# Second attention's scores and values and the pooling's grouped projection as three passes of split operands

## The chip, the cores and the metric

The kernel runs on one core of a Trainium2 chip. The metric is the time on the device of one execution, in microseconds: 1687.03 as the median of three runs (1686.83 to 1687.77). Lower is better.

## The reference, cut to what matters

Two transformer layers follow each other over 256 tokens of width 2048, all in f32. The change touches two parts of the second layer: the windowed attention's two products, and the linear map of the pooling branch.

```python
def windowed_gqa(q, k, v, rel_table, sink):      # 8 query heads, 2 key heads, width 128
    ...
    logits = jnp.einsum('bnqkgd,bntkd->bnkgqt', qb, kw).astype(jnp.float32) * (HEAD_DIM_2 ** -0.5)
    ...
    probs = jax.nn.softmax(jnp.concatenate([logits, sink_l], axis=-1), axis=-1)[..., :-1]
    out = jnp.einsum('bnkgqt,bntkd->bnqkgd', probs.astype(vw.dtype), vw)

def multiscale_pool(u, w_grp, scale):            # 4 groups of 256 channels, windows 2, 4, 8, 16
    ...
    pooled = jnp.stack(outs, axis=2).astype(u.dtype)
    mixed = jnp.einsum('bsgc,gcd->bsgd', pooled, w_grp).reshape(B, S, POOL_WIDTH)
    return mixed * scale

def hybrid_layer(...):
    proj = h @ w_in
    q, k, v, gate_a, u, gate_p = jnp.split(proj, SPLIT_POINTS, axis=-1)
    y_a = windowed_gqa(q, k, v, rel_table, sink) * jax.nn.silu(gate_a)
    y_p = multiscale_pool(u, w_pool_grp, pool_scale) * jax.nn.silu(gate_p)
    ...
```

## The kernel before, in words

All large products read f32 weights from HBM. A "sub" is a piece of 256 rows by 512 columns of one weight matrix. SyncE loads it (tile `raw`, 8 buffers); ScalarE copies it into the reduced format f32r (`w_hi`, 4 buffers, L1158); VectorE subtracts that copy from it (`w_lo`, L1442); and TensorE multiplies in three passes, high by high, high by low and low by high (L726 and its neighbours). The activations have been split in the same way (`X_pair`, `Y_pair`).

Five phases follow each other: P1 (first layer's mixing), P2 (its MLP), P3 (second layer's input projection, 72 subs in nine blocks of eight), P4 (merge) and P5 (output). In P3 each sub is 24 passes of 256 columns into the PSUM tile `G`, whose two halves take the blocks in turn. Between the subs stand small "stages" that use the other PSUM tile, `S`. The list `STAGES` gives each a slot (after which sub it comes) and the number of steps that each engine has in it. Each engine walks the same list by itself: at slot s, ScalarE and VectorE first convert sub s + 3 (`AHEAD` = 3) and then do their part of the stages of slot s, strictly in order; TensorE multiplies sub s and then does its part. A w_hi can be written when TensorE is done with the sub four before it. `enter` makes an engine wait until all other engines have finished all steps of the stages that stand before this one in the list.

The stages that matter here, by slot:

- `inb0` (7), `inb1` (15), then `inb2`, `inb3` with the second and third score stage (24, 31), `inb4` (40): ScalarE copies a finished block out of `G`: keys and values, queries (two blocks), pooling inputs `u` (two blocks). `inb5` (47) is a Silu of the attention's gate.
- `gate_sum` (8): small matmuls of the gate vector.
- Four rounds (half of the tokens by four heads each): `win_L` (17, 24, 31, 38), the scores, L1104, then scaling, bias and maximum on VectorE; `win_E` the exponentials on ScalarE; `win_M` the sum on VectorE; `win_S` (five slots after win_L), eight transposes of the probabilities into two banks of `S` (L707), one bank copied out by ScalarE (L1382) and one by VectorE (L1793) side by side; `win_V` (one slot later), the values, L1117, copied to `ya` (L1804).
- `pool_0` to `pool_3` (45, 46, 47, 49): window sums on VectorE (L1816 to L1825). GpSimd loads the group weights `w_grp` (1 MB) when it enters pool_0.
- `pool_W` (53): the grouped projection, sixteen f32 matmuls of 256 columns, L1124; it waits for `w_grp`.

A plain f32 matmul is one instruction in the program:

```python
ins = nc.tensor.matmul(S[:, k // 2, TOK * (k % 2):TOK * (k % 2 + 1)],
                       q2_T[:, h0 + k, P * tt:P * (tt + 1)], k2_T[:, (h0 + k) // 4, :], start=True, stop=True)
```

The profile leaves out buffer numbers in names: q2_T is q_T there, v2 is v, probs2_T is probs_T.

Of the kernel before, what the change touches and what calls it, by code (L numbers as in the profile page):

```python
# [27 lines left out]
P = 128  # L28
# [240 lines left out]
stage("P3", 0, "h2_scale", D=4)  # L269
for _k in range(4):  # L270
    stage("P3", 2 + _k, f"h2_T{_k + 1}", P=1, A=1, D=2)
stage("P3", 7, "inb0", A=1)
stage("P3", 8, "gate_sum", P=1, D=1)
stage("P3", 9, "gate_row", P=1, D=1)
stage("P3", 10, "x_fin0", D=1)
stage("P3", 12, "x_fin1", D=1)
stage("P3", 15, "inb1", A=1)
stage("P3", 16, "u_pads", G=1)
for _g, _s in enumerate((17, 24, 31, 38)):
    stage("P3", _s, f"win_L{_g}", P=1, D=4)  # L280
    if _g in (1, 2):
        stage("P3", _s, f"inb{_g + 1}", A=1)
    stage("P3", _s + 2, f"win_E{_g}", A=2)
    if _g == 3:
        stage("P3", 40, "inb4", A=1)
    stage("P3", _s + 3, f"win_M{_g}", D=3)
    stage("P3", _s + 5, f"win_S{_g}", P=1, A=1, D=1)
    stage("P3", _s + 6, f"win_V{_g}", P=1, D=1)
stage("P3", 45, "pool_0", D=3)
stage("P3", 46, "pool_1", D=4)  # L290
stage("P3", 47, "pool_2", D=5)
stage("P3", 47, "inb5", A=1)
stage("P3", 49, "pool_3", D=6)
stage("P3", 53, "pool_W", P=1, A=1, D=1)
stage("P3", 55, "inb6", A=1)
stage("P3", 56, "ya0", A=1, D=2)
stage("P3", 57, "ya1", A=1, D=2)
# [51 lines left out]
def program(nc, t, out):  # L349
# [4 lines left out]
    with ctx:  # L354
# [89 lines left out]
        y_n, _ = put("y_n", X_AT, [P, NT, D_MODEL])  # L444
        tmp_T, _ = put("tmp_T", X_AT + 16 * KB, [P, 4, NW])
        bias2, at2 = put("bias2", X_AT, [P, NT, Q_HEADS2, TOK])
        q2_T, at2 = put("q2_T", at2, [P, Q_HEADS2, TOK])
        k2_T, at2 = put("k2_T", at2, [P, KV_HEADS2, TOK])
        probs2, at2 = put("probs2", at2, [P, 4, TOK])
        w_grp, _ = put("w_grp", X_AT + 16 * KB, [P, 4, 2, PGW])  # L450
        assert at2 <= X_AT + 32 * KB
        ya, at = put("ya", AR, [P, Q_HEADS2, TOK])
        v2, at = put("v2", at, [P, NT, KV_HEADS2 * P])
        probs2_T, at = put("probs2_T", AR + 12 * KB, [P, 4, 2, P])
        ga, at = put("ga", at, [P, 8, TOK])
        yp, _ = put("yp", at, [P, 8, TOK])
        u, at = put("u", at, [P, 8, PAD + TOK + PAD])
        gp, at = put("gp", at, [P, 8, TOK])
        sums, at = put("window_sums", at, [P, 2, 2, PAD + TOK + PAD])
        assert at <= AR + 48 * KB  # L460
        pool_edge, _ = put("pool_edge", AR + 10 * KB, [P, 4, 2, PAD])

        sig, at = put("sig", AR, [P, 2, 4, TOK])
# [241 lines left out]
        def _(pe):  # L705
# [90 lines left out]
                need("P1", OUT_AT + 10 + k, "D", step("D", "mix_T2", k + 1))  # L796
            need("P1", OUT_AT + 16, "D", done("D", "out0"))
            need("P1", OUT_AT + 24, "D", done("D", "out1"))
            for b in range(9):
                if b >= 2:  # L800
                    need("P3", 8 * b, "A", done("A", f"inb{b - 2}"))
            for k in range(8):
                need("P3", k, "D", halves_made(2 * k) if k < 4 else done("D", f"h2_T{k - 3}"))
            need("P5", 0, "G", done("G", "br_p", QUARTERS - 2))
# [102 lines left out]
            def stages(name, i):  # L907
# [158 lines left out]
                elif name == "gla_F":  # L1066
                    for tt in range(NT):
                        for h in range(GLA_HEADS):
                            ins = nc.tensor.matmul(S[:, tt, P * h:P * (h + 1)], ki_T[:, tt, h, :], qd_T[:, tt, h, :],
                                                   start=True, stop=True)  # L1070
                    ins.then_inc(pe_side, 1)
                elif name[:5] == "gla_G":
                    for h in range(GLA_HEADS):
                        v = 2 * GW + GLA_DV * h
                        for n in ((0, 1) if name == "gla_G01" else (2,)):
                            tt, r = n // 2, slice(GLA_CHUNK * (n % 2), GLA_CHUNK * (n % 2 + 1))
                            b0 = 2 * ((n + 1) % 2)
                            ins = nc.tensor.matmul(S[0:GLA_DK, b0 + h // 2, GLA_DV * (h % 2):GLA_DV * (h % 2 + 1)],
                                                   gla[r, tt, GW + GLA_DK * h:GW + GLA_DK * (h + 1)],
                                                   gla[r, tt, v:v + GLA_DV], start=True, stop=True)  # L1080
                    ins.then_inc(pe_side, 1)
                elif name == "gla_O":
                    for tt in range(NT):
                        for h in range(GLA_HEADS):
                            v = 2 * GW + GLA_DV * h
                            c_ = slice(GLA_DV * (h % 2), GLA_DV * (h % 2 + 1))
                            b_ = 2 * tt + h // 2
                            nc.tensor.matmul(S[:, b_, c_], sc_T[:, tt, h, :], gla[:, tt, v:v + GLA_DV],
                                             start=h % 2 == 0, stop=False, skip_group_check=True)
                    for n, h in [(n, h) for h in range(GLA_HEADS) for n in (1, 2)] + [(3, h) for h in range(GLA_HEADS)]:  # L1090
                        tt, r = n // 2, slice(GLA_CHUNK * (n % 2), GLA_CHUNK * (n % 2 + 1))
                        c_ = slice(GLA_DV * (h % 2), GLA_DV * (h % 2 + 1))
                        ins = nc.tensor.matmul(S[r, 2 * tt + h // 2, c_], qd_T[:, tt, h, r], state[:, n - 1, h, :],
                                               start=False, stop=True, skip_group_check=True)
                    ins.then_inc(pe_side, 1)
                elif name == "gate_sum":
                    fold(S[:, 0, 0:KC], 2 * KC, KC)
                elif name == "gate_row":
                    swap(S[0:KC, 1, 0:P], gate_v[:, :]).then_inc(pe_side, 1)
                elif name[:5] == "win_L":  # L1100
                    g = int(name[-1])
                    tt, h0 = g % 2, 4 * (g // 2)
                    for k in range(4):
                        ins = nc.tensor.matmul(S[:, k // 2, TOK * (k % 2):TOK * (k % 2 + 1)],  # L1104
                                               q2_T[:, h0 + k, P * tt:P * (tt + 1)], k2_T[:, (h0 + k) // 4, :],
                                               start=True, stop=True)
                    ins.then_inc(pe_side, 1)
                elif name[:5] == "win_S":
                    for k in range(4):
                        for kt in range(2):  # L1110
                            ins = swap(S[:, k // 2, TOK * (k % 2) + P * kt:TOK * (k % 2) + P * (kt + 1)],
                                       probs2[:, k, P * kt:P * (kt + 1)])
                    ins.then_inc(pe_side, 1)
                elif name[:5] == "win_V":
                    g = int(name[-1])
                    for kt in range(2):
                        ins = nc.tensor.matmul(S[:, 2, :], v2[:, kt, P * (g // 2):P * (g // 2 + 1)], probs2_T[:, :, kt, :],  # L1117
                                               start=kt == 0, stop=kt == 1)
                    ins.then_inc(pe_side, 1)
                elif name == "pool_W":  # L1120
                    pe.wait_ge(grp_in, 16)
                    for k in range(8):
                        for c in range(2):
                            ins = nc.tensor.matmul(S[:, k // 2, TOK * (k % 2):TOK * (k % 2 + 1)],  # L1124
                                                   w_grp[:, k // 2, c, P * (k % 2):P * (k % 2 + 1)],
                                                   u[:, 2 * (k // 2) + c, PAD:PAD + TOK], start=c == 0, stop=c == 1)
                    ins.then_inc(pe_side, 1)
                else:
                    raise AssertionError(name)
# [13 lines left out]
        def _(act):  # L1143
# [44 lines left out]
            def stages(name, i):  # L1188
# [41 lines left out]
                elif name[:3] == "inb":  # L1230
# [3 lines left out]
                    G1 = G[:, (b + 1) % 2, 1, :].rearrange("p (c q) -> p c q", q=TOK)  # L1234
                    both = G[:, (b + 1) % 2, :, :].rearrange("p a (c q) -> p (a c) q", q=TOK)
                    if b == 0:
                        nc.scalar.activation(k2_T[:, :, :], G0, ACT.Copy)
                        ins = nc.scalar.activation(v2[:, :, :], G1, ACT.Copy)
                    elif b < 3:
                        ins = nc.scalar.activation(q2_T[:, 4 * (b - 1):4 * b, :], both, ACT.Copy)  # L1240
                    elif b < 5:
                        ins = nc.scalar.activation(u[:, 4 * (b - 3):4 * (b - 2), PAD:PAD + TOK], both, ACT.Copy)
                    else:
# [135 lines left out]
                    nc.scalar.activation(small[:, 48:52], small[:, 24:28], ACT.Exp).then_inc(act_side, 1)  # L1379
                elif name[:5] == "win_S":  # L1380
                    act.wait_ge(pe_side, done("P", name))
                    nc.scalar.activation(probs2_T[:, 0:2, :, :], S[:, 0, :].rearrange("p (h k q) -> p h k q", h=2, k=2),  # L1382
                                         ACT.Copy).then_inc(act_side, 1)
                elif name == "pool_W":
                    act.wait_ge(pe_side, done("P", name))
                    nc.scalar.activation(yp[:, 0:4, :], S[:, 0:2, :].rearrange("p a (c q) -> p (a c) q", q=TOK),
# [44 lines left out]
        def _(dve):  # L1431
# [83 lines left out]
            def stages(name, i):  # L1515
# [274 lines left out]
                                        bias2[:, g % 2, h0:h0 + 4, ::-1])], probs2[:, :, :], 4, SWA_HEADS + h0, HD2 ** -0.5)  # L1790
                elif name[:5] == "win_S":
                    dve.wait_ge(pe_side, done("P", name))
                    nc.vector.tensor_copy(probs2_T[:, 2:4, :, :], S[:, 1, :].rearrange("p (h k q) -> p h k q", h=2, k=2)  # L1793
                                          ).then_inc(dve_side, 1)
                elif name[:5] == "win_M":
                    softmax_sum(name, 4)
                    dve.wait_ge(dve_side, step("D", name, 2))
# [215 lines left out]
```

## Time and profile before

| what | value |
|---|---|
| device time, median of 3 runs | 1687.03 us |
| span of the profiled execution | 1685.6 us |
| the profiled execution's own device time | not given apart from its span |
| TensorE busy | 1676.8 us (99%) |
| VectorE busy | 1121.0 us (67%) |
| ScalarE busy | 822.0 us (49%) |
| HBM read over the span | 358.00 MB, 214 GB/s |
| P3, about | 1093 to 1324 us |

The span runs from the first to the last instruction in the trace. Busy times are those of an engine's instructions; TensorE's weight loads (PEld) are counted by themselves and lie beside its matmuls. A matmul's record is longer than its share of the engine, since matmuls are pipelined: the distance from one start to the next tells what it costs. A plain f32 matmul is two records.

### The profile page before, as it was taken

The page shows a single profiled execution, that of the slowest core. Times are in us where ns is not written, and L with a number is a line of the kernel's source. Part 1 is how long each engine was busy: PE and PEld are TensorE (multiplying, and loading weights), DVE is VectorE, ACT ScalarE, POOL GpSimd, SP SyncE. Part 2 cuts the span into 40 slices and gives each one's busy share as a digit, 9 for nine tenths or more (in the row PEclk, how much of TensorE's full clock was granted, in tenths as well). Part 3 has the DMA queues.
Part 4 walks back from the last instruction along what each step waited for, and adds up shares of the span by engine and source line. Part 5 has one row for each costly group of instructions (what it writes and reads, how often), then busy time and mean ns, then how long its engine had stood idle before and what let it go on. Part 6 is the DMA issues. An engine that isn't in the chain of part 4 may idle for free.

```text
span 1685.6 us, 25429 instructions
## 1 busy us (share of the span) xinstructions
PE 1676.8 (99%) x9373; PEld 1453.1 (86%) x9373; DVE 1121.0 (67%) x1143; ACT 822.0 (49%) x1084; POOL 56.3 (3%) x63
## 2 busy tenths in 40 slices
PE   9999999999999999999999999999999999999998
PEld 6888888888888888888888888799999988888886
DVE  5454546557877777777877777775575566757754
ACT  5645754554445444454455445454444454444443
POOL 1000000000000000000000000000000001101100
PEclk9999999999999999999999999999999999999999
DMA  8643545467777788767777777675555655555562
GB/s 299 220 136 116 188 138 173 163 206 267 261 257 262 271 277 278 252 233 277 267 265 258 267 254 259 209 243 159 169 169 176 193 189 191 179 195 173 195 205 88
DMA packets 171643, 361.47 MB, mean 214 GB/s; under 512 B 10971, under 2 KB 17435, under 8 KB 171296
## 3 DMA queue, kind: packets, MB, share of 16 engines
q1 hardware_dynamic: 169376, 352.37, 62.7%
q0 software_dynamic: 2032, 7.56, 1.2%
q8 instruction: 65, 1.06, 0.3%
q10 hardware_dynamic: 144, 0.26, 0.0%
q14 instruction: 26, 0.21, 0.0%
HBM read 358.00 MB, written 2.15 MB: 214 GB/s over the span
## 4 chain that ended last, share of the span: by engine, by line
PE 98%; DVE 1%; issue 1%; ACT 0%; POOLq 0%; POOL 0%; ACTq 0%; DVEq 0%
PE G L745 31%; PE S L745 13%; PE S L759 12%; PE G L759 12%; PE G L726 10%; PE G L762 6%; PE S L762 6%; PE S L707 2%; PE G L732 1%; PE S L1124 0%; PE S L1104 0%; PE S L1117 0%; PE S L778 0%; DVE window_sums L1816 0%; PE S L993 0%
## 5 line engine op out<-in xcount | busy, mean ns | idle before, releaser
L1442 DVE TENSOR_TENSOR w_lo<-raw,w_hi 128x1024 fp32r<-128x1024 f32 (+2 forms) x574 | 704.4, 1245 | 414.9 <-ACT w_hi L1158 414.1
L1158 ACT ACTIVATE w_hi<-raw 128x1024 fp32r<-128x1024 f32 (+2 forms) x575 | 589.5, 1045 | 522.3 <-PE G L745 130.7
L745 PE MATMUL G<-w_hi,X_pair 128*128 128x512 f32 (+2 forms) x1472 | 450.0, 384 | 0.1
L745 PEld LDWEIGHTS G<-w_hi,X_pair 128*128 128x128 f32 x1472 | 272.5, 188 | 56.2 <-issue 3.7
L745 PE MATMUL G<-w_lo,X_pair 128*128 128x512 f32 (+2 forms) x736 | 280.0, 380 | 0.0
L759 PE MATMUL S<-Y_pair,w_hi 128*128 128x512 f32 x768 | 267.0, 390 | 0.0
L759 PE MATMUL G<-Y_pair,w_hi 128*128 128x512 f32 x768 | 266.8, 390 | 0.0
L762 PE MATMUL G<-Y_pair,w_lo 128*128 128x256 f32 x768 | 216.6, 282 | 0.0
L762 PE MATMUL S<-Y_pair,w_lo 128*128 128x256 f32 x768 | 216.6, 282 | 0.0
L726 PE MATMUL G<-Y_pair,w_hi 128*128 128x256 f32 x1088 | 196.2, 283 | 1.1 <-DVE Y_pair L1558 0.9
L759 PEld LDWEIGHTS S<-Y_pair,w_hi 128*128 128x128 f32 x768 | 144.1, 188 | 30.3
L759 PEld LDWEIGHTS G<-Y_pair,w_hi 128*128 128x128 f32 x768 | 144.1, 188 | 30.2
L726 PEld LDWEIGHTS G<-Y_pair,w_hi 128*128 128x128 f32 x1088 | 166.3, 188 | 3.7 <-issue 1.9
L745 PEld LDWEIGHTS G<-w_lo,X_pair 128*128 128x128 f32 x736 | 138.4, 188 | 25.8 <-issue 0.5
L745 PE MATMUL S<-w_hi,X_pair 128*128 128x512 f32 x512 | 158.3, 389 | 0.0
L726 PE MATMUL G<-Y_pair,w_lo 128*128 128x256 f32 x544 | 151.7, 279 | 0.0
L762 PEld LDWEIGHTS S<-Y_pair,w_lo 128*128 128x128 f32 x768 | 145.1, 189 | 0.2
L762 PEld LDWEIGHTS G<-Y_pair,w_lo 128*128 128x128 f32 x768 | 145.2, 189 | 0.0
L1455 DVE SCALAR_TENSOR_TENSOR ada_acc<-ada_w,c_silu,ada_acc 128x768 f32<-128x768 f32 x120 | 121.5, 1012 | 0.0
L745 PEld LDWEIGHTS S<-w_hi,X_pair 128*128 128x128 f32 x512 | 96.1, 188 | 20.0
L726 PEld LDWEIGHTS G<-Y_pair,w_lo 128*128 128x128 f32 x544 | 102.2, 188 | 0.0
L745 PE MATMUL S<-w_lo,X_pair 128*128 128x512 f32 x256 | 99.6, 389 | 0.0
(334 smaller groups left out, 1429.0 us busy)
## 6 DMA issues: line engine op xcount, KB each, us to landing
raw<-in_w_in SPq DMA_DIRECT2D x143, 512.0 KB, 4.4
raw<-in_w_mlp_in SPq DMA_DIRECT2D x128, 512.0 KB, 5.4
raw<-in_w_mlp_out SPq DMA_DIRECT2D x128, 512.0 KB, 6.7
ada_w<-in_w_ada SPq DMA_DIRECT2D x64, 768.0 KB, 4.9
raw<-in_w_out SPq DMA_DIRECT2D x64, 512.0 KB, 4.5
raw<-in_w_merge SPq DMA_DIRECT2D x64, 512.0 KB, 4.2
raw<-in_w_branch_attn SPq DMA_DIRECT2D x16, 512.0 KB, 4.1
raw<-in_w_branch_pool SPq DMA_DIRECT2D x16, 512.0 KB, 6.0
```

What stands on the lines that cost most here:

```text
L707: return nc.tensor.transpose(out_, in_, ident)
L726: ins = nc.tensor.matmul(G[:, bank, j // 2, TOK * (j % 2):TOK * (j % 2 + 1)], w[:, s % SPLIT, c, cut], a[:, c0 + c, :], start=first and c ...
L732: ins = nc.tensor.matmul(G[:, bank, 1, TOK * tt:TOK * (tt + 1)], a[:, c0 + c, P * tt:P * (tt + 1)], w[:, s % SPLIT, c, P * turned:NW], sta ...
L745: ins = nc.tensor.matmul(token_bank(bank, tt)[:, 0:n], a[:, c0 + c, tok], w[:, s % SPLIT, c, 0:n], start=first and c == 0 and k == 0, stop ...
L759: nc.tensor.matmul(bank, w_hi[:, s % SPLIT, c, cut], both[:, c0 + c, :, :].rearrange("p a q -> p (a q)"), start=first and c == 0, stop=Fal ...
L762: ins = nc.tensor.matmul(bank[:, 0:TOK], w_lo[:, s % SPLIT, c, cut], both[:, c0 + c, 0, :], start=False, stop=last and c == SUB - 1, skip_ ...
L1158: nc.scalar.activation(w_hi[:, s % SPLIT, :, 0:n], raw[:, k, :, 0:n], ACT.Copy).then_inc(hi_ready, 1)
L1442: nc.vector.tensor_tensor(w_lo[:, s % SPLIT, :, 0:n], raw[:, k, :, 0:n], w_hi[:, s % SPLIT, :, 0:n], ALU.subtract).then_inc(lo_ready, 1)
L1455: nc.vector.scalar_tensor_tensor(a, w, cs[:, v:v + 1], a, ALU.mult, ALU.add).then_inc(ada_free, 1)
```

## The change

The f32 operands of these products are replaced by pairs of f32r tiles, high and low, and each f32 matmul by three passes. ScalarE's copies out of PSUM now write the high tiles, and VectorE gets a step in `inb0`, `inb1` and `inb2` that subtracts them for the low ones. In `win_S` ScalarE copies both banks, and VectorE then subtracts; before, each copied one. Three stages are new: `pool_w` (48) splits the group weights (2048 elements per partition on each engine), `pool_u0` (51) and `pool_u1` (53) split the pooled inputs. `pool_W` moves from slot 53 to 55, and the wait for the load of `w_grp` from TensorE to ScalarE's pool_w. TensorE's blocks 2, 3 and 4 now wait for VectorE's step of the drain. The new tiles lie on space that is free at that time.

```diff
-stage("P3", 7, "inb0", A=1)
+stage("P3", 7, "inb0", A=1, D=1)
...
-stage("P3", 15, "inb1", A=1)
+stage("P3", 15, "inb1", A=1, D=1)
...
-        stage("P3", _s, f"inb{_g + 1}", A=1)
+        stage("P3", _s, f"inb{_g + 1}", A=1, D=2 - _g)
...
+stage("P3", 48, "pool_w", A=1, D=1)
 stage("P3", 49, "pool_3", D=6)
-stage("P3", 53, "pool_W", P=1, A=1, D=1)
+stage("P3", 51, "pool_u0", A=1, D=1)
+stage("P3", 53, "pool_u1", A=1, D=1)
+stage("P3", 55, "pool_W", P=1, A=1, D=1)
...
-            for b in range(9):
-                if b >= 2:
-                    need("P3", 8 * b, "A", done("A", f"inb{b - 2}"))
+            for b in range(2, 9):
+                need("P3", 8 * b, "D" if b < 5 else "A", done("D" if b < 5 else "A", f"inb{b - 2}"))
...
-                        ins = nc.tensor.matmul(S[:, k // 2, TOK * (k % 2):TOK * (k % 2 + 1)],
-                                               q2_T[:, h0 + k, P * tt:P * (tt + 1)], k2_T[:, (h0 + k) // 4, :],
-                                               start=True, stop=True)
+                        for m, (q, keys) in enumerate(((q2_hi, k2_hi), (q2_hi, k2_lo), (q2_lo, k2_hi))):
+                            ins = nc.tensor.matmul(S[:, k // 2, TOK * (k % 2):TOK * (k % 2 + 1)],
+                                                   q[:, h0 + k, P * tt:P * (tt + 1)], keys[:, (h0 + k) // 4, :],
+                                                   start=k % 2 == 0 and m == 0, stop=m == 2, skip_group_check=True)
...
-                        ins = nc.tensor.matmul(S[:, 2, :], v2[:, kt, P * (g // 2):P * (g // 2 + 1)], probs2_T[:, :, kt, :],
-                                               start=kt == 0, stop=kt == 1)
+                        for m, (v, p) in enumerate(((v2_hi, probs2_hi), (v2_hi, probs2_lo), (v2_lo, probs2_hi))):
+                            ins = nc.tensor.matmul(S[:, 2, :], v[:, kt, P * (g // 2):P * (g // 2 + 1)], p[:, :, kt, :],
+                                                   start=kt == 0 and m == 0, stop=kt == 1 and m == 2)
...
-                    pe.wait_ge(grp_in, 16)
                     for k in range(8):
                         for c in range(2):
+                            for m, (w, a) in enumerate(((w_grp_hi, u_hi), (w_grp_lo, u_hi), (w_grp_hi, u_lo))):
...
-                    nc.scalar.activation(probs2_T[:, 0:2, :, :], S[:, 0, :].rearrange("p (h k q) -> p h k q", h=2, k=2),
+                    nc.scalar.activation(probs2_hi[:, :, :, :].rearrange("p (a h) k q -> p a (h k q)", a=2), S[:, 0:2, :],
...
+                elif name == "pool_w":
+                    act.wait_ge(grp_in, 16)
+                    nc.scalar.activation(w_grp_hi[:, :, :, :], w_grp[:, :, :, :], ACT.Copy).then_inc(act_side, 1)
+                elif name in ("pool_u0", "pool_u1"):
+                    k = 4 * int(name[-1])
+                    nc.scalar.activation(u_hi[:, k:k + 4, :], u[:, k:k + 4, PAD:PAD + TOK], ACT.Copy).then_inc(act_side, 1)
...
-                    nc.vector.tensor_copy(probs2_T[:, 2:4, :, :], S[:, 1, :].rearrange("p (h k q) -> p h k q", h=2, k=2)
-                                          ).then_inc(dve_side, 1)
+                    dve.wait_ge(act_side, done("A", name))
+                    nc.vector.tensor_tensor(probs2_lo[:, :, :, :].rearrange("p (a h) k q -> p a (h k q)", a=2), S[:, 0:2, :],
+                                            probs2_hi[:, :, :, :].rearrange("p (a h) k q -> p a (h k q)", a=2),
+                                            ALU.subtract).then_inc(dve_side, 1)
...
+                elif name == "pool_w":
+                    dve.wait_ge(act_side, done("A", name))
+                    nc.vector.tensor_tensor(w_grp_lo[:, :, :, :], w_grp[:, :, :, :], w_grp_hi[:, :, :, :],
+                                            ALU.subtract).then_inc(dve_side, 1)
...
```

VectorE's steps of `inb0` to `inb2`, `pool_u0` and `pool_u1` have the form of the last one: wait for ScalarE's step, subtract.

## Rows read from the trace of the kernel before

**Rows 1.** The page: busy time by engine; the chain of waits by engine.
```profile
PE 1676.8 (99%) x9373; PEld 1453.1 (86%) x9373; DVE 1121.0 (67%) x1143; ACT 822.0 (49%) x1084; POOL 56.3 (3%) x63
...
PE 98%; DVE 1%; issue 1%; ACT 0%; POOLq 0%; POOL 0%; ACTq 0%; DVEq 0%
```

**Rows 2.** Four stretches: us, busy by engine (instructions), PE clock, DMA share, GB/s.
```profile
1148.00:1172.00 24.00, 24.00 (x191) 22.83 (x190) 13.78 (x20) 11.25 (x18) 0.00 (x0) 1.00 0.56 171
1244.00:1254.00 10.00, 10.00 (x88) 10.00 (x87) 8.67 (x14) 2.56 (x3) 0.05 (x1) 1.00 0.82 262
1679.00:1680.00 1.00, 0.00 (x0) 0.00 (x0) 0.69 (x2) 0.08 (x1) 0.56 (x1) 1.00 0.09 33
1683.00:1684.00 1.00, 0.00 (x0) 0.00 (x0) 0.00 (x0) 0.00 (x0) 0.00 (x0) 0.50 1.06 367
```

**Rows 3.** Chain of waits in order of time: start, us, engine, line, count.
```profile
1043.98 43.52 PE G L745 x192
...
1119.39 2.79 PE G L726 x24
...
1148.43 1.73 PE S L1104 x8
...
1165.03 2.81 PE G L726 x24
1167.84 1.72 PE S L1117 x4
...
1267.31 6.91 PE S L1124 x32
```

**Rows 4.** Timeline of PE: start, us, weight loads (PEld) or matmuls, [idle before].
```profile
1167.56 0.31 PEld L1117 LDWEIGHTS S<-probs_T,v 128*128 128x128 f32 x2
...
1264.24 0.30 PEld L726 LDWEIGHTS G<-Y_pair,w_hi 128*128 128x128 f32 x2 [0.41 <-DVE w_lo L1442]
...
1680.38 1.13 PE L1139 MATMUL S<-o_sb,diag 128*128 128x512 f32 x2 [1.52 <-ACT diag L1410]
```

**Rows 5.** Timeline of ACT, attention and pooling.
```profile
1120.00 0.59 ACT L1238 ACTIVATE v<-G 128x512 f32<-128x512 f32 x1
...
1165.15 0.60 ACT L1382 ACTIVATE probs_T<-S 128x512 f32<-128x512 f32 x1 [2.63 <-PE S L707]
...
1254.86 1.03 ACT L1245 ACTIVATE ga<-G 128x1024 f32<-128x1024 f32 x1
1255.78 3.89 ACT L1158 ACTIVATE w_hi<-raw 128x1024 fp32r<-128x1024 f32 x4
```

**Rows 6.** Timeline of DVE, the same stretch.
```profile
1213.30 0.69 DVE L1793 COPY probs_T<-S 128x512 f32<-128x512 f32 x1 [0.76 <-PE S L707]
...
1256.87 2.36 DVE L1442 TENSOR_TENSOR w_lo<-raw,w_hi 128x1024 fp32r<-128x1024 f32 x2 [3.44 <-ACT w_hi L1158]
1259.15 0.72 DVE L1816 TENSOR_TENSOR window_sums<-u 128x542 f32<-128x542 f32 x1
...
1262.97 4.62 DVE L1442 TENSOR_TENSOR w_lo<-raw,w_hi 128x1024 fp32r<-128x1024 f32 x4
```

**Rows 7.** Groups by shape, ACT and DVE: count | busy us, mean ns | idle before.
```profile
L1158 ACT ACTIVATE w_hi<-raw 128x1024 fp32r<-128x1024 f32 x559 | 579.9, 1056 | 516.7 <-PE S L762 126.3 <-PE G L745 125.1 <-PE G L762 119.1
...
L1158 ACT ACTIVATE w_hi<-raw 128x512 fp32r<-128x512 f32 x8 | 4.7, 640 | 2.5 <-PE G L745 2.5
...
L1442 DVE TENSOR_TENSOR w_lo<-raw,w_hi 128x512 fp32r<-128x512 f32 x8 | 5.3, 688 | 5.5 <-ACT w_hi L1158 5.5
...
L1488 DVE SCALAR_TENSOR_TENSOR probs<-S,bias 128x1024 f32<-128x1024 f32 x4 | 4.9, 1226 | 10.5 <-PE S L1104 10.5
...
L1767 DVE SCALAR_TENSOR_TENSOR x_res<-x_res,stat,norm_f 128x2048 f32<-128x2048 f32 x2 | 4.7, 2344 | 0.0
```

**Rows 8.** The load of w_grp: KB, us to landing; its issue on POOL.
```profile
w_grp<-in_w_pool_group POOLq DMA_DIRECT2D x1, 1024.0 KB, 8.0
...
1243.13 0.92 POOL L1897 DMA_DIRECT2D w_grp<-in_w_pool_group  x1 [98.85 <-DVE ya L1804]
```

More of the change, by code:

```diff
@@ L446, in program @@
         bias2, at2 = put("bias2", X_AT, [P, NT, Q_HEADS2, TOK])
-        q2_T, at2 = put("q2_T", at2, [P, Q_HEADS2, TOK])
-        k2_T, at2 = put("k2_T", at2, [P, KV_HEADS2, TOK])
+        q2_hi, at2 = put("q2_hi", at2, [P, Q_HEADS2, TOK], f32r)
+        k2_hi, at2 = put("k2_hi", at2, [P, KV_HEADS2, TOK], f32r)
+        k2_lo, at2 = put("k2_lo", at2, [P, KV_HEADS2, TOK], f32r)
         probs2, at2 = put("probs2", at2, [P, 4, TOK])
+        w_grp_hi, _ = put("w_grp_hi", X_AT, [P, 4, 2, PGW], f32r)
+        w_grp_lo, _ = put("w_grp_lo", X_AT + 8 * KB, [P, 4, 2, PGW], f32r)
         w_grp, _ = put("w_grp", X_AT + 16 * KB, [P, 4, 2, PGW])
@@ L452, in program @@
         ya, at = put("ya", AR, [P, Q_HEADS2, TOK])
-        v2, at = put("v2", at, [P, NT, KV_HEADS2 * P])
-        probs2_T, at = put("probs2_T", AR + 12 * KB, [P, 4, 2, P])
+        v2_hi, at = put("v2_hi", at, [P, NT, KV_HEADS2 * P], f32r)
+        probs2_hi, at = put("probs2_hi", AR + 12 * KB, [P, 4, 2, P], f32r)
         ga, at = put("ga", at, [P, 8, TOK])
@@ L457, in program @@
         u, at = put("u", at, [P, 8, PAD + TOK + PAD])
+        q2_lo, _ = put("q2_lo", at, [P, Q_HEADS2, TOK], f32r)
+        u_hi, _ = put("u_hi", at, [P, 8, TOK], f32r)
         gp, at = put("gp", at, [P, 8, TOK])
         sums, at = put("window_sums", at, [P, 2, 2, PAD + TOK + PAD])
+        v2_lo, at = put("v2_lo", at, [P, NT, KV_HEADS2 * P], f32r)
         assert at <= AR + 48 * KB
+        probs2_lo, _ = put("probs2_lo", AR + 16 * KB, [P, 4, 2, P], f32r)
+        u_lo, _ = put("u_lo", X_AT + 24 * KB, [P, 8, TOK], f32r)
         pool_edge, _ = put("pool_edge", AR + 10 * KB, [P, 4, 2, PAD])
@@ L1116, in stages @@
                     for kt in range(2):
-                        ins = nc.tensor.matmul(S[:, 2, :], v2[:, kt, P * (g // 2):P * (g // 2 + 1)], probs2_T[:, :, kt, :],
-                                               start=kt == 0, stop=kt == 1)
+                        for m, (v, p) in enumerate(((v2_hi, probs2_hi), (v2_hi, probs2_lo), (v2_lo, probs2_hi))):
+                            ins = nc.tensor.matmul(S[:, 2, :], v[:, kt, P * (g // 2):P * (g // 2 + 1)], p[:, :, kt, :],
+                                                   start=kt == 0 and m == 0, stop=kt == 1 and m == 2)
                     ins.then_inc(pe_side, 1)
                 elif name == "pool_W":
-                    pe.wait_ge(grp_in, 16)
                     for k in range(8):
                         for c in range(2):
-                            ins = nc.tensor.matmul(S[:, k // 2, TOK * (k % 2):TOK * (k % 2 + 1)],
-                                                   w_grp[:, k // 2, c, P * (k % 2):P * (k % 2 + 1)],
-                                                   u[:, 2 * (k // 2) + c, PAD:PAD + TOK], start=c == 0, stop=c == 1)
+                            for m, (w, a) in enumerate(((w_grp_hi, u_hi), (w_grp_lo, u_hi), (w_grp_hi, u_lo))):
+                                ins = nc.tensor.matmul(S[:, k // 2, TOK * (k % 2):TOK * (k % 2 + 1)],
+                                                       w[:, k // 2, c, P * (k % 2):P * (k % 2 + 1)], a[:, 2 * (k // 2) + c, :],
+                                                       start=k % 2 == 0 and c == 0 and m == 0, stop=c == 1 and m == 2,
+                                                       skip_group_check=True)
                     ins.then_inc(pe_side, 1)
@@ L1236, in stages @@
                     if b == 0:
-                        nc.scalar.activation(k2_T[:, :, :], G0, ACT.Copy)
-                        ins = nc.scalar.activation(v2[:, :, :], G1, ACT.Copy)
+                        nc.scalar.activation(k2_hi[:, :, :], G0, ACT.Copy)
+                        ins = nc.scalar.activation(v2_hi[:, :, :], G1, ACT.Copy)
                     elif b < 3:
-                        ins = nc.scalar.activation(q2_T[:, 4 * (b - 1):4 * b, :], both, ACT.Copy)
+                        ins = nc.scalar.activation(q2_hi[:, 4 * (b - 1):4 * b, :], both, ACT.Copy)
                     elif b < 5:
@@ L1792, in stages @@
                     dve.wait_ge(pe_side, done("P", name))
-                    nc.vector.tensor_copy(probs2_T[:, 2:4, :, :], S[:, 1, :].rearrange("p (h k q) -> p h k q", h=2, k=2)
-                                          ).then_inc(dve_side, 1)
+                    dve.wait_ge(act_side, done("A", name))
+                    nc.vector.tensor_tensor(probs2_lo[:, :, :, :].rearrange("p (a h) k q -> p a (h k q)", a=2), S[:, 0:2, :],
+                                            probs2_hi[:, :, :, :].rearrange("p (a h) k q -> p a (h k q)", a=2),
+                                            ALU.subtract).then_inc(dve_side, 1)
+                elif name in ("inb0", "inb1", "inb2"):
+                    b = int(name[3:])
+                    dve.wait_ge(act_side, done("A", name))
+                    both = G[:, (b + 1) % 2, :, :].rearrange("p a (c q) -> p (a c) q", q=TOK)
+                    if b == 0:
+                        nc.vector.tensor_tensor(k2_lo[:, :, :], both[:, 0:2, :], k2_hi[:, :, :], ALU.subtract)
+                        ins = nc.vector.tensor_tensor(v2_lo[:, :, :], both[:, 2:4, :], v2_hi[:, :, :], ALU.subtract)
+                    else:
+                        q = slice(4 * (b - 1), 4 * b)
+                        ins = nc.vector.tensor_tensor(q2_lo[:, q, :], both, q2_hi[:, q, :], ALU.subtract)
+                    ins.then_inc(dve_side, 1)
+                elif name == "pool_w":
+                    dve.wait_ge(act_side, done("A", name))
+                    nc.vector.tensor_tensor(w_grp_lo[:, :, :, :], w_grp[:, :, :, :], w_grp_hi[:, :, :, :],
+                                            ALU.subtract).then_inc(dve_side, 1)
+                elif name in ("pool_u0", "pool_u1"):
+                    dve.wait_ge(act_side, done("A", name))
+                    k = 4 * int(name[-1])
+                    nc.vector.tensor_tensor(u_lo[:, k:k + 4, :], u[:, k:k + 4, PAD:PAD + TOK], u_hi[:, k:k + 4, :],
+                                            ALU.subtract).then_inc(dve_side, 1)
                 elif name[:5] == "win_M":
```

## Prediction

> **What bounds the kernel now.** First the busy shares and the chain of waits: TensorE (PE) is busy 99% of the span and makes up 98% of the chain [rows 1]. So time goes only where PE has less to stream, and comes where PE is made to wait. The change lies in the third phase (P3), whose matmuls are 72 "subs" of 24 passes of 256 columns; ScalarE (ACT) makes each sub's w_hi, VectorE (DVE) its w_lo, three subs ahead. The stretches show how much room the helpers have there: in one attention round DVE works 13.8 of 24 us and ACT 11.3, but in the 10 us in which the pooling sums start DVE works 8.7 of 10 [rows 2]. The third view is the timeline around that place. PE has its one wait for w_lo of this phase at 1263.8: weight loads that follow each other by 0.12 us stop and go on at 1264.24, released by DVE [rows 4]. There PE has no slack: it is sub 53, just before the pooling's projection (pool_W). A microsecond more on DVE or ACT in front of that w_lo is a microsecond of PE. The reader is to see both sides: whatever the change saves on PE is certain, whatever it adds to DVE between 1244 and 1263 is paid.
>
> **What PE saves.** In before a plain f32 matmul appears as two records. Eight records of 256 columns (scores, four matmuls) take 1.73 us, four of 512 columns (values, two matmuls) 1.72, and the 32 of pool_W 6.91 [rows 3]. A split pass of 256 columns costs 2.81/24 = 0.117 us, one of 512 columns 43.52/192 = 0.227 [rows 3]. Three passes instead of one f32 product then are:
> scores, 12 passes: 1.41 us, 0.32 less, four times: 1.29;
> values, 6 passes: 1.36 us, 0.36 less, four times: 1.44;
> pool_W, 48 passes: 5.63 us, 1.28 less.
> Together 4.0 us. The small gain on three passes against two double records comes from the pass itself: half a record is 6.91/64 = 0.108 us, a split pass 0.117. Bounds: if a pass cost only that 0.108, the sum would be 12 × 0.108 = 1.30 per scores round and so on, 5.0 us in all; if the first pass after another kind of work lost another 0.1 us in each of the nine places, 3.1. I take 4.0, since the passes are of the very form that surrounds them.
> The Trainium skill ("FP8 and Floating Point Precision", TensorE Precision Notes) says that true FP32 takes four passes through the array; three for four would save a quarter of 1.73 × 4 + 1.72 × 4 + 6.91 = 20.7 us, 5.2 us. By that rule alone the net below would be 2.3 us faster instead of 1.2; the rows, where a lone pass costs more than a quarter of an f32 product, decide.
>
> **What is added where it is hidden.** (1) Block drains inb0 to inb2: DVE now subtracts behind ACT's copies, two of 512 elements (0.69 us each) and two of 1024 (1.23) [rows 7]. inb0 is the nearest: ACT's copy ends at 1120.59 [rows 5], the two subtractions by 1121.9, and PE's next side stage, gate_sum, which now waits for them too, follows sub 8 at 1122.18 [rows 3]; 0.25 us to spare. inb1 has two subs (5.6 us) before the first scores, for 1.03 + 1.23. inb2 waits behind the softmax maximum as its copy did already. What is queued behind, w_lo for three subs ahead, moves by 0.2 to 0.3. If such a cover is gone, PE waits the difference once. Bounds 0 and 0.3; I take 0. PE's own new waits (blocks 2 to 4 on DVE) come eight subs after the drain: nothing.
> (2) win_S, four times: today ACT and DVE each copy 512 elements of the turned probabilities side by side; now ACT copies 1024 (1.03, as q_T and ga) and DVE subtracts 1024 after it (1.23). From the end of the transposes at 1165.03: ACT starts 1165.15 [rows 5], ends 1166.18, DVE 1166.21 to 1167.43. PE wants the result when the loads of the values begin, 1167.56 [rows 4]. The handoff DVE to PE took 0.05 in the wait above, so 0.08 us is left. DVE is free at that time (0.76 idle before the copy where it was least [rows 6]) and the next w_hi and w_lo behind it have three subs of room. Bounds: 0, and 4 × 0.2 = 0.8 us lost if each handoff is 0.1 to 0.3 longer. I take 0.
> (3) pool_u0, pool_u1: 1024 each on ACT and DVE, in slots 51 and 53, ahead of pool_W, now in slot 55. ACT's first waits for pool_3, and w_hi of sub 55 is queued behind it: see the next part.
> (4) The load of w_grp starts as before at 1243.13 and lands 8.0 us later, 1251.1 [rows 8]; its reader is now ACT at 1256.7, not PE at 1267: 5.6 us of room.
>
> **What is added in front of the tight place.** pool_w sits in slot 48: ACT copies 2048 elements, DVE subtracts them after, and on DVE this stands ahead of w_lo 52, pool_3 and w_lo 53. ACT: pool_2's end lets the gate's activation run at 1254.86, w_hi 51 starts 1255.78, the next 0.94 later [rows 5]: so pool_w starts at 1256.72. A copy of 512 takes 0.640, of 1024 1.056, so one of 2048 1.89 [rows 7]: end 1258.61. DVE starts it at 1258.64, where before it started w_lo 52 at 1256.87 + 1.13 = 1258.00 [rows 6]: 0.64 idle. The subtraction: 0.688 for 512, 1.226 for 1024, so 2.30 for 2048 (a 2048-wide row took 2.34), less 0.09 that neighbours overlap: 2.21 [rows 7]. Everything behind is 0.64 + 2.21 = 2.85 us later. w_lo 52 is made at 1262.1 and PE wanted it at about 1261.0: 1.1 lost. pool_3 follows, 3.82 from its start to that of w_lo 53 (1259.15 to 1262.97 [rows 6]), and w_lo 53 ends at 1267.0 instead of 1264.2: PE has waited 2.85 more in all, since it was already waiting here. Bounds: 2.2 if the copy on ACT costs DVE no idle time, 3.5 if pool_w takes 0.3 more on each engine. I take 2.85.
> What is late next: w_lo 54 follows at 1268.2, wanted 1269.9. pool_u0 on ACT starts at pool_3's end, 1265.9; w_hi 55 ends 1268.0, DVE does w_lo 54, pool_u0, w_lo 55 (done 1270.5, wanted 1272.7), w_lo 56 and pool_u1 by 1272.8; pool_W wants that at 1275.5. Nothing more is lost. The weights' loads keep five subs of room. These instants are on before's clock; attention ends 2.7 us earlier, but pool_0 is started by the values of round four and so the whole place moves with PE.
>
> **The sum.** −4.0 + 2.85 = −1.15 us. The page gives for the profiled execution its span, 1685.6; the runs' median, 1687.03, holds 1.4 us more around it, which the change doesn't touch. 1687.03 − 1.15 = 1685.9.
>
> **Rivals.**
> A, the pool place is free after all: the gain stands whole, 1687.0 − 4.0 = 1683.0. It needs DVE to have 2.85 us before 1263; against it are its 8.7 of 10 and PE's wait. 0.11.
> B, win_S becomes the bound of each round: 0.1 to 0.3 late four times, 1686.3 to 1687.1. For it: only 0.08 us of room. 0.12.
> C, slower: the stall lowers PE's clock. PE would stand still 1.1 us, run sub 52, and stand 2.1 us. At the kernel's end the granted clock is 1.00 with PE idle at 1679, and is 0.50, the 1.2 GHz level, at 1683, after the last matmuls' end at 1681.5 [rows 2, 4]; between them PE ran only two records. If it fell here, each sub at 1.2 GHz costs 2.81 more: one sub makes 1685.9 + 2.8 = 1688.7, two 1691.5. It decides from 1.15 us, ten passes at the lower level. Against it: the clock stayed at 1.00 through the 1.5 us wait that ended at 1680.38 [rows 4], and sub 52 is dense between the two stalls. 0.07. The Trainium skill ("TensorE: Matmul & The Clock Gate", HAM oscillation) warns of a re-throttle after long idle gaps; no row before the end shows one.
> D, slower: w_grp comes late. ACT, in order, would hold all w_hi behind pool_w; each microsecond after 1256.7 is lost, and from 1257.9 (14.7 us after issue) the kernel is slower than before. Landing twice as late as today, 1259.1, makes 1688.3. Against: the same load at the same place took 8.0. 0.04. The Trainium skill ("SBUF — State Buffer", the "DVE blocks DMA" trap) has descriptors of a GpSimd DMA held up by DVE copies; the 8.0 us stand with DVE 8.7 of 10 busy, so the row doesn't show it.
> That it doesn't do what it says is no case here: every f32 product named goes.
>
> **Chances.** Forecast 0.66, likeliest from 1684.9 to 1686.8 (stall 2.2 to 3.5, saving 3.7 to 4.3). About 0.2% of this time, 3.4 us, is what a measurement can tell: 1683.7 and below is faster (A: 0.11, and 0.02 of the forecast), 1690.4 and above slower (two subs at the lower clock, a very late load: 0.05). Same 0.82. The range takes in B, one slow sub nearly, and leaves out A: 1683.9 to 1688.3.
>
> **What would show it.** Twelve single passes 0.12 us apart at each scores round, where eight records stood; each round's scores 1.4, values 1.36, pool_W 5.6. PE waits for w_lo twice in P3's pooling, 1.1 and about 2.2 to 2.5; before it all is 2.7 us earlier than now. DVE's subtraction of w_grp starts when ACT's copy ends. Wrong would be: no wait of PE, or a third before pool_W; a wait in front of the values of over 0.1; a granted clock under 1.00 after 1260; ACT waiting for a DMA at pool_w.

## The result and the profile after

The changed kernel takes 1689.99 us (median of 20 runs, 1687.77 to 1690.44), the kernel before 1687.3 (20 runs, 1686.33 to 1688.04): ratio 1.0014, 95% interval 1.0008 to 1.0020. It is 2.7 us slower, where 1.15 us faster was forecast. Its profiled execution has a span of 1688.1 us against 1685.6. Nearly all of the 2.5 us between the spans lies in P3: from its first pass to the first pass of P4 it is 231.02 us before (1093.45 to 1324.47) and 233.37 after, 2.35 more. This length of P3 is the ruler below. It comes from one profiled execution of each kernel, and it leaves out what stands ahead of P3, which varies: P3 starts between 1092.78 and 1093.95 us in the ten profiles.

The busy shares (engine, busy us, share, instructions) hardly move: TensorE's matmuls are still at 99% [rows 1], with 0.3 us less busy time in spite of a longer span.

```profile
PE 1676.5 (99%) x9413; PEld 1456.4 (86%) x9413; DVE 1130.6 (67%) x1150; ACT 827.3 (49%) x1087; POOL 56.4 (3%) x63
```

The stretches around the pooling show more than a stall (columns as in [rows 2]: us, busy of PE, PEld, DVE, ACT, POOL with counts, PE's granted clock, DMA share, GB/s).

```profile
1260.00:1262.00 2.00, 1.24 (x10) 1.25 (x11) 1.97 (x3) 0.00 (x0) 0.00 (x0) 1.00 0.22 19
1262.00:1264.00 2.00, 1.85 (x16) 1.64 (x14) 1.86 (x5) 0.00 (x0) 0.00 (x0) 1.00 0.70 243
1264.00:1266.00 2.00, 0.29 (x2) 0.30 (x3) 2.00 (x3) 1.31 (x2) 0.00 (x0) 1.00 0.00 0
1266.00:1268.00 2.00, 2.00 (x13) 2.00 (x13) 2.00 (x3) 1.64 (x2) 0.00 (x0) 0.56 0.53 112
1268.00:1270.00 2.00, 2.00 (x12) 2.00 (x12) 2.00 (x2) 1.06 (x1) 0.00 (x0) 0.58 1.02 373
1270.00:1272.00 2.00, 2.00 (x19) 2.00 (x18) 1.80 (x3) 1.06 (x1) 0.00 (x0) 1.00 0.86 253
```

PE stands still twice, and behind the second wait it is "busy" for 4 us with 12 or 13 matmuls in 2 us where 19 is usual: the granted clock has gone to its lower level, 1.2 GHz. The means of 0.56 and 0.58 make 3.4 us at that level. The matmuls show both waits, and the passes at the lower clock, 0.64 us for three where three take 0.35 otherwise; the last line is the first pass of sub 54, so sub 53 took 4.47 us:

```profile
1260.76 0.50 PE L737 MATMUL G<-Y_pair,w_hi 128*128 128x256 f32 x2 [1.01 <-DVE w_lo L1461]
...
1265.70 0.50 PE L737 MATMUL G<-Y_pair,w_hi 128*128 128x256 f32 x2 [1.86 <-DVE w_lo L1461]
...
1267.35 0.63 PE L737 MATMUL G<-Y_pair,w_hi 128*128 128x256 f32 x2
1267.77 0.41 PE L737 MATMUL G<-Y_pair,w_lo 128*128 128x256 f32 x1
1267.99 0.63 PE L737 MATMUL G<-Y_pair,w_hi 128*128 128x256 f32 x2
...
1270.17 0.40 PE L737 MATMUL G<-Y_pair,w_hi 128*128 128x256 f32 x2
```

VectorE's timeline shows the cause of the waits, in the order that the prediction gave (answers to [rows 6]): the subtraction of the group weights, then w_lo of sub 52, pool_3, w_lo of sub 53.

```profile
1257.27 2.29 DVE L1829 TENSOR_TENSOR w_grp_lo<-w_grp,w_grp_hi 128x2048 fp32r<-128x2048 f32 x1 [0.68 <-ACT w_grp_hi L1399]
1259.48 1.22 DVE L1461 TENSOR_TENSOR w_lo<-raw,w_hi 128x1024 fp32r<-128x1024 f32 x1
1260.62 0.72 DVE L1857 TENSOR_TENSOR window_sums<-u 128x542 f32<-128x542 f32 x1
...
1264.43 2.35 DVE L1461 TENSOR_TENSOR w_lo<-raw,w_hi 128x1024 fp32r<-128x1024 f32 x2
```

In the attention each round's values should follow sub s + 6 at once. ScalarE's copy, VectorE's subtraction and the weight loads (PEld) show a gap instead (answers to [rows 4, 5]):

```profile
1165.06 1.03 ACT L1395 ACTIVATE probs_hi<-S 128x1024 fp32r<-128x1024 f32 x1 [2.66 <-PE S L718]
```

```profile
1166.22 1.23 DVE L1813 TENSOR_TENSOR probs_lo<-S,probs_hi 128x1024 fp32r<-128x1024 f32 x1 [2.56 <-ACT probs_hi L1395]
```

```profile
1167.36 0.19 PEld L737 LDWEIGHTS G<-Y_pair,w_lo 128*128 128x128 f32 x1
1167.67 0.19 PEld L1129 LDWEIGHTS S<-probs_hi,v_hi 128*128 128x128 f32 x1
1167.78 0.19 PEld L1129 LDWEIGHTS S<-probs_lo,v_hi 128*128 128x128 f32 x1
```

The loads come every 0.12 us, but the first load of the values comes 0.31 behind the one before it, 0.19 late: it waits for VectorE's result, which ends at 1167.45. The projection itself takes less time, in the chain of waits (start, us; answers to the last row of [rows 3]):

```profile
1276.09 5.77 PE S L1136 x48
```

### The profile page after: what moved, and what is told of

Read it like the earlier page. It is cut to its first block and busy times, and to the rows that moved or that the text cites. A ratio compares the mean times of both kernels' runs of the same rounds, so it can differ in the third digit from the quotient of the medians.

```text
span 1688.1 us, 25541 instructions
## 1 busy us (share of the span) xinstructions
PE 1676.5 (99%) x9413; PEld 1456.4 (86%) x9413; DVE 1130.6 (67%) x1150; ACT 827.3 (49%) x1087; POOL 56.4 (3%) x63
```

## The experiments

Each experiment has its own 33 runs of the kernel before beside it (median 1687.45 us for experiments 1 to 4, 1686.98 for 5 to 8); P3's length is from its one profiled execution.

**1. The attention half alone.** The stages and the product of the pooling are as before.

```diff
-stage("P3", 48, "pool_w", A=1, D=1)
 stage("P3", 49, "pool_3", D=6)
-stage("P3", 51, "pool_u0", A=1, D=1)
-stage("P3", 53, "pool_u1", A=1, D=1)
-stage("P3", 55, "pool_W", P=1, A=1, D=1)
+stage("P3", 53, "pool_W", P=1, A=1, D=1)
...
+pe.wait_ge(grp_in, 16)
...
-for m, (w, a) in enumerate(((w_grp_hi, u_hi), (w_grp_lo, u_hi), (w_grp_hi, u_lo))):
...
+    w_grp[:, k // 2, c, ...], u[:, 2 * (k // 2) + c, PAD:PAD + TOK], ...
```

> Only the attention half of the change; the pooling's projection stays one f32 product in slot 53. Theory (from the trace after the change): scores save about 0.3 us a round, values only about 0.1 because their first pass waits for VectorE's subtraction, together 1.5 us: 1685.8. Rival (the forecast): scores and values save 2.7 us: 1684.6. Under both PE has the one wait of before ahead of sub 53 (0.2 us) and the granted clock stays 1.00.

Measured: 1685.89 us (1685.56 to 1686.46, 11 runs) against 1687.45, ratio 0.9993 (0.9983 to 1.0002); P3 1.64 us shorter. The interval takes in no difference, but the slowest of these runs is faster than the fastest of the kernel before (1686.53). The theory from the trace holds, the forecast's 2.7 does not: the attention half gives 1.6.

**2. The pooling half alone.** The kernel before with the three new stages and the split projection.

```diff
+stage("P3", 48, "pool_w", A=1, D=1)
 stage("P3", 49, "pool_3", D=6)
-stage("P3", 53, "pool_W", P=1, A=1, D=1)
+stage("P3", 51, "pool_u0", A=1, D=1)
+stage("P3", 53, "pool_u1", A=1, D=1)
+stage("P3", 55, "pool_W", P=1, A=1, D=1)
... (the tiles, the steps and the three passes as in the changed kernel)
```

> Only the pooling half: w_grp and u split, three passes in slot 55; attention as before. Theory: 2.95 us of stall ahead of subs 52 and 53, 1.15 us saved in pool_W, 0.25 lost before sub 60: 2.0 slower than before, 1689.3 where the clock stays, and 1.7 to 1.9 more, 1691.1, in executions in which it falls to 1.2 GHz after the second stall. Rival (the stall costs only itself and the forecast sum of this half holds): +2.85 - 1.28 = 1.6 slower, 1688.9, in all executions, with one level of times.

Measured: 1690.66 us (1689.48 to 1691.21), 3.2 more than before; P3 4.17 longer. The lower clock is in its profile too (same columns as above):

```profile
1267.00:1268.00 1.00, 1.00 (x11) 1.00 (x10) 1.00 (x2) 1.00 (x2) 0.00 (x0) 1.00 0.58 45
1268.00:1269.00 1.00, 1.00 (x7) 1.00 (x7) 1.00 (x2) 0.55 (x2) 0.00 (x0) 0.54 0.73 252
```

The halves add up to within 0.2 us: -1.64 + 4.17 = 2.53 us of P3 against 2.35 of the whole. So little arises from their meeting, and the loss is in the pooling half. The times don't fall into two clear levels here, so the 1689.3 expected for executions without the lower clock was seen at most once (1689.48).

**3. Idle work in both waits.** In the changed kernel TensorE runs passes that nothing reads while it would wait.

```diff
+                    if ph == "P3" and local in {52: 3, 53: 7}:
+                        for _ in range({52: 3, 53: 7}[local]):
+                            nc.tensor.matmul(S[:, 3, :], y_hi[:, 0, 0:P], y_pair[:, 0, :, :].rearrange("p a q -> p (a q)"),
+                                             start=True, stop=True)
```

> The changed kernel, with TensorE given idle work while it waits: three extra 512-column passes into a free PSUM bank ahead of sub 52 (0.7 of the 1.1 us stall) and seven ahead of sub 53 (1.6 of 2.1 us). They add nothing to the result. Theory (the lowered clock costs about 1.8 us by itself): granted clock 1.00 throughout, all executions at the lower of the two levels seen, 1688.0, 2 us under the changed kernel's usual 1690.0. Rival (the lowered clock is a symptom and what it delays would wait anyway): 1690.0 as before, whatever the clock shows.

Measured: 1688.31 us (1687.97 to 1688.98, 11 runs), P3 1.61 us shorter than the changed kernel's. Its matmuls and one stretch:

```profile
1263.74 1.78 PE L854 MATMUL S<-Y_pair 128*128 128x512 f32 x7
...
1265.75 0.51 PE L737 MATMUL G<-Y_pair,w_hi 128*128 128x256 f32 x2 [0.23 <-DVE w_lo L1465]
...
1268.66 0.40 PE L737 MATMUL G<-Y_pair,w_hi 128*128 128x256 f32 x2
```

```profile
1266.00:1268.00 2.00, 2.00 (x19) 2.00 (x19) 2.00 (x3) 1.69 (x2) 0.00 (x0) 1.00 0.52 120
```

Sub 53 starts at the same moment as in the changed kernel (1265.75 and 1265.70), because VectorE is as late; only what PE did just before differs. It then runs 19 matmuls in 2 us instead of 13, and sub 54 starts at 1268.66 instead of 1270.17: sub 53 takes 2.91 us instead of 4.47. This isolates the clock: 1.56 us.

**4. The same work in other slots.**

```diff
-stage("P3", 48, "pool_w", A=1, D=1)
 stage("P3", 49, "pool_3", D=6)
 stage("P3", 51, "pool_u0", A=1, D=1)
-stage("P3", 53, "pool_u1", A=1, D=1)
-stage("P3", 55, "pool_W", P=1, A=1, D=1)
+stage("P3", 53, "pool_w", A=1, D=1)
+stage("P3", 54, "pool_u1", A=1, D=1)
 stage("P3", 55, "inb6", A=1)
-stage("P3", 56, "ya0", A=1, D=2)
-stage("P3", 57, "ya1", A=1, D=2)
+stage("P3", 58, "pool_W", P=1, A=1, D=1)
+stage("P3", 60, "ya0", A=1, D=2)
+stage("P3", 61, "ya1", A=1, D=2)
```

> The changed kernel with the same added work in other slots: pool_3 49, pool_u0 51, pool_w 53, pool_u1 54, pool_W 58, ya0 and ya1 60 and 61. Theory (the stall comes from pool_w standing in front of pool_3 and w_lo of sub 53, not from the amount of work): PE waits before sub 53 as in the kernel before (0.2 to 0.4 us) and nowhere else, clock 1.00: before minus 1.5 (attention) minus 1.15 (projection) = 1684.7, to 1685.2 if a small wait is left. Rival (VectorE is full in this stretch and its 4.5 us of new work is paid wherever it stands): a stall of about 3 us at a later sub, 1687.9 or more.

Measured: 1684.77 us (11 runs) against 1687.45, ratio 0.9987 (0.9978 to 0.9996). P3 is 4.79 us shorter than the changed kernel's and 2.44 shorter than before. PE has again one wait for w_lo, before sub 53, as in [rows 4]; the gap in front of the values is still there (experiment 5):

```profile
1263.11 0.30 PEld L737 LDWEIGHTS G<-Y_pair,w_hi 128*128 128x128 f32 x2 [0.40 <-DVE w_lo L1461]
```

The work was not too much for VectorE; it stood in front of the wrong things.

**5. win_S in two halves,** on the attention half alone (code shortened, comments added).

```diff
-stage("P3", _s + 5, f"win_S{_g}", P=1, A=1, D=1)
+stage("P3", _s + 5, f"win_S{_g}", P=1, A=2, D=1)
...
+for a in range(2):      # ScalarE: copy bank a, step a + 1
+    nc.scalar.activation(probs2_hi[:, 2 * a:2 * a + 2, :, :], S[:, a, :]..., ACT.Copy).then_inc(act_side, 1)
...
+for a in range(2):      # VectorE: subtract bank a behind it
+    dve.wait_ge(act_side, step("A", name, a + 1))
...
```

> The attention half alone, with win_S in two halves: ScalarE copies bank 0, then bank 1; VectorE subtracts bank 0 while bank 1 is being copied. The low probabilities are then ready about 1.95 us after the transposes instead of 2.3. Theory (values wait for VectorE's subtraction): no gap before the values, 0.15 to 0.2 us saved in each of four rounds, 1685.2 against 1685.9 of the attention half alone. Rival (the missing 0.25 us per round lie in the passes themselves, for example in the first pass after the switch of PSUM banks): 1685.9 unchanged, and the gap in front of the values stays at 0.3 us.

Measured: 1684.98 us (11 runs) against 1686.98, ratio 0.9988 (0.9978 to 0.9997), a difference of 2.0 where the attention half alone had 1.56; P3 0.59 us shorter than there, 0.15 a round. VectorE's pair (start 1165.51, done 1166.80) and the loads, now without a gap:

```profile
1165.51 1.29 DVE L1811 TENSOR_TENSOR probs_lo<-S,probs_hi 128x512 fp32r<-128x512 f32 x2 [2.13 <-ACT probs_hi L1392]
```

```profile
1167.07 0.19 PEld L734 LDWEIGHTS G<-Y_pair,w_lo 128*128 128x128 f32 x1
1167.19 0.19 PEld L1126 LDWEIGHTS S<-probs_hi,v_hi 128*128 128x128 f32 x1
1167.31 0.19 PEld L1126 LDWEIGHTS S<-probs_lo,v_hi 128*128 128x128 f32 x1
```

**6 and 7. Idle work in one wait only:** `{52: 3}` and `{53: 7}` in the edit of experiment 3.

> The changed kernel with three extra 512-column passes ahead of sub 52 only, so that PE idles 0.3 to 0.4 us there and 2.1 us ahead of sub 53. Theory A (the longer idle time decides the clock): it still falls to 1.2 GHz behind sub 53's wait, 1690.0. Theory B (both idle times together decide, PE idle 3.2 us out of 6): the clock stays, 1688.3.

> The changed kernel with seven extra passes ahead of sub 53 only: PE idles 1.1 to 1.2 us ahead of sub 52 and 0.4 ahead of sub 53. Theories A and B both: the clock stays at 1.00, 1688.3. If it falls all the same, a stall of 1.1 us is enough, and the time is 1690.

Measured: with the first wait filled 1690.0 us (11 runs, 1687.62 to 1690.27), and the clock falls in the profile; with the second filled 1688.34 (1687.65 to 1688.85), and it stays. One row of each:

```profile
1266.00:1268.00 2.00, 2.00 (x13) 2.00 (x13) 2.00 (x3) 1.64 (x2) 0.00 (x0) 0.59 0.52 112
```

```profile
1266.00:1268.00 2.00, 2.00 (x19) 2.00 (x19) 2.00 (x3) 1.73 (x2) 0.00 (x0) 1.00 0.43 96
```

The longer wait is the one that matters (theory A): with it filled none of 22 executions (experiments 3 and 7) is at the slower level. But it doesn't decide alone: of the eleven executions with the first wait filled, five took 1687.6 to 1688.0 (mean granted clock 0.999 or 1.000) and six 1690.0 to 1690.3 (0.998), with nothing between. The changed kernel's twenty have the same two levels: five at 1687.77 to 1688.53, all with a mean granted clock of 1.000, and fifteen at 1689.73 to 1690.44 with 0.998 or 0.999. The program alone doesn't decide whether the clock falls after such a wait. Whether filling the first wait made the fall rarer (6 of 11 against 15 of 20) can't be told from so few.

**8. All of it together:** experiment 4 with pool_3 in slot 50, pool_u0 in 52, and the halves of experiment 5.

> All that the runs so far point to: the late pooling stages with pool_3 in slot 50 and pool_u0 in 52 (so that w_lo of sub 53 is made ahead of pool_3), and win_S in two halves. Theory: no wait of PE for w_lo in the pooling (0.45 less than the late version) and none in front of the values (4 times 0.15 to 0.2): 1684.8 - 1.1 = 1683.7. Rival (the waits only move on to sub 54 and to the values' own passes): 1684.8.

Measured: 1683.69 us (1683.39 to 1684.38, 11 runs) against 1686.98, ratio 0.9982 (0.9973 to 0.9991): 3.3 us faster than before, and faster than the changed kernel. P3 is 3.63 shorter than before. PE has no wait for w_lo, on a VectorE as full as in the changed kernel (23.88 of these 30 us in both; 19.22 in the kernel before):

```profile
1244.00:1254.00 10.00, 10.00 (x88) 10.00 (x88) 6.41 (x11) 4.26 (x5) 0.00 (x0) 1.00 0.64 212
1254.00:1264.00 10.00, 10.00 (x88) 10.00 (x87) 9.74 (x12) 5.97 (x7) 0.00 (x0) 1.00 0.50 162
1264.00:1274.00 10.00, 10.00 (x88) 10.00 (x87) 7.73 (x6) 6.81 (x7) 0.00 (x0) 1.00 0.65 208
```

VectorE works 9.74 of 10 us in the middle stretch and nothing waits, since what PE needs soon stands ahead of the long work.

## Why the prediction was wrong, point by point

**The sum lacked the clock.** The first step that failed is the sum, -4.0 + 2.85: it priced a stall at its own length and the clock at nothing. Rival C, with 0.07, was what happened in 15 of 20 executions, by their times and mean granted clocks. It cost 1.56 us: sub 53 took 4.47 us at the fallen clock and 2.91 in experiment 3, whose P3 is 1.61 shorter. The 3.4 us at the lower level hold about sixteen passes, 0.213 us apart instead of 0.117. The argument against it, that the clock had stayed at 1.00 through a 1.5 us wait [rows 4], took a shorter wait for a longer one: the second stall was 2.1 us, and filling it brought the clock back. The other argument, a dense sub 52 between the stalls, didn't protect it either. Rival C's price, 2.81 a sub, was too high for what was seen: a pass at the lower clock costs 0.213 us, not twice 0.117, and the clock rose again within sub 53. The Trainium skill ("TensorE: Matmul & The Clock Gate", HAM oscillation) warns of a re-throttle after idle gaps longer than any here; in this case a gap of 2.1 us was enough in most executions, so the measurement is the stricter one and decides.

**What TensorE saves was too large.** The second step that failed is the 4.0: 2.78 was there, 1.64 in the attention half and 1.14 in the projection. Without the clock the kernel would still have been slower, not 1.15 us faster. What a product costs is read here from the starts of the 256-column passes before and behind it. Scores: 1.72 us before and 1.44 after, 0.28 a round where 0.32 was forecast. Values: 1.71 and 1.55, 0.16 a round where 0.36 was forecast. This is rival B (0.12): the 0.08 us of room in win_S were none. VectorE ended at 1167.45, close to what was worked out (1167.43), but the load followed at 1167.67, 0.22 later, where the handoff behind w_lo was 0.04. Experiment 5 gave 0.59 us of P3 back and brought the values to 1.38, near the forecast 1.36. Why this handoff is longer is open: the waits of `enter` are several and PE's queue runs ahead of the loads, but that was not tried. pool_W: forecast 1.28; 48 passes took 5.77 instead of 6.91, 1.14, since a pass took 0.120 and not 0.117. The forecast's upper bound, 5.0, had a slip: with 0.108 a quarter everywhere its own rule gives 5.2.

**Not all that was hidden stayed hidden.** inb0 was given 0.25 us to spare and the value 0 out of 0 to 0.3; it cost 0.14, once. TensorE's loads before and at gate_sum, in the kernel before:

```profile
1121.80 0.19 PEld L726 LDWEIGHTS G<-Y_pair,w_lo 128*128 128x128 f32 x1
1122.11 0.29 PEld L896 LDWEIGHTS S<-mats,b_ada 48*128 48x128 f32 x2
```

The same two after, and VectorE's second subtraction of inb0:

```profile
1121.95 0.19 PEld L737 LDWEIGHTS G<-Y_pair,w_lo 128*128 128x128 f32 x1
1122.40 0.29 PEld L906 LDWEIGHTS S<-mats,b_ada 48*128 48x128 f32 x2 [0.26 <-issue]
```

```profile
1121.49 0.68 DVE L1822 TENSOR_TENSOR v_lo<-G,v_hi 128x512 fp32r<-128x512 f32 x1
```

The two loads stand 0.45 us apart instead of 0.31, and the second comes 0.23 after VectorE's end at 1122.17: the same long handoff as in front of the values. All runs with the attention half have this gap, experiment 2 doesn't. With it the attention half comes to 4 × 0.28 + 4 × 0.16 - 0.14 = 1.62, against 1.64 measured. inb1 and inb2 cost nothing visible: no round's scores start late. The load of w_grp landed 8.0 us after issue as before; rival D didn't occur.

**The stall was right.** Forecast 2.85 in all, 1.1 and then 2.2 to 2.5. Attention's last copy moved by -1.49 (1241.77 to 1240.28) and w_lo 53 by +1.46 (1262.97 to 1264.43): 2.95. Both waits are where they were put, 1.2 and 2.1 us by the weight loads' idle time (1.0 and 1.9 by the matmuls'), with VectorE idle 0.68 before the subtraction (forecast 0.64) and 2.29 in it (2.30). "Nothing more is lost" was a little wrong: PE waited once more, 0.28, at 1296.06, behind ya0 and ya1, which now meet the copies of the later pool_W.

**The ledger of P3:** -1.64 attention, +2.95 stall, -1.14 projection, +1.56 clock, +0.28 the late wait, and passes that came further apart than 0.117: 48 of subs 54 and 55 at 0.120, +0.16, and about 118 behind the projection, up to that late wait, at 0.118, +0.13. Together +2.3, against 2.35 measured. With the clock left out the same ledger gives +0.7, which is what the five executions at the clock's upper level show (1687.77 to 1688.53, median 1688.01, against 1687.3): even these are not faster, though most of them lie inside the forecast's range, and that is luck, not its mechanism. Against the forecast of -1.15 the 3.45 us missing are the clock 1.56, the savings 1.22, the wider passes 0.29, the late wait 0.28 and the stall 0.1. Rival A's wish, the gain whole, needs another order of the stages, and experiment 8 has most of it: 3.3 of 4.0 us.

## What to carry to other kernels

On an engine that is 99% busy, a saving on it is safe, but each wait that helpers add in front of it counts in full, and more: price a wait of TensorE of 2 us with the passes behind it at 1.2 GHz as well (here 1.56 us more). Where TensorE goes over to a stage that waits for another engine's last result, leave more than 0.2 us of room; 0.04 was too little to reckon with. Before adding work to a helper, find the operation that the bound engine already waits for, and put the new work behind it; the same work in other slots turned +2.7 us into -2.7. Where a copy becomes a copy and then a subtraction, cut it in halves, so that the second engine starts when the first half is there.

## What the runs showed of the hardware that was not expected

The clock fell from 2.4 to 1.2 GHz after TensorE had waited 1.2 us, run 2.8 us densely and waited 2.1 us, and rose again 3.4 us later, in dense work. It fell too in 6 of 11 executions with the first wait filled; it never did with the second filled to 0.4 us, and it stayed in a quarter of the executions of one and the same program.

Two 256-column passes of one form don't always follow each other at the same distance. In long stretches of P3 it is 0.1167 us or 0.1178, in both kernels, and it changes where a stage or a wait stands between the subs: in the kernel before it is 0.1178 from 1126 to 1148 us and 0.1167 from 1242 to 1262. It is 0.120 in the split projection in every run, and in subs 54 and 55 of the changed kernel alone. Behind the split projection it is 0.1178 in every run, in experiments 4 and 8 to the end of P3, which costs about 0.3 us there. The lower clock doesn't bring the 0.120: in experiment 6 the clock fell as well, and subs 54 and 55 kept 0.1167. What does, no run here shows.

A handoff from VectorE to TensorE took 0.04 us behind a w_lo but 0.22 in front of the values and 0.23 in front of gate_sum.
